# Token rows into expert order: indirect transfers and transposes in place of one-hot products

## What is computed

```python
x = _layernorm(DN_ALPHA * x + mod[2] * mixer(h), ln_g[l, 0], ln_b[l, 0])
h = x * (1.0 + mod[4]) + mod[3]
gsel = argmax(h @ w_group + b_group)                       # one group per token
top_p, top_i = top_k(softmax(elog of that group), 2)       # two experts in it
comb = sum(one_hot(eid, 32) * gw * top_p)
hid = silu(h @ w_gate[e]) * (h @ w_up[e]) * comb
moe = sum over e of hid @ w_down[e]
x = _layernorm(DN_ALPHA * x + mod[5] * moe, ln_g[l, 1], ln_b[l, 1])
```

## Time and profile before

| | us |
|---|---|
| median of three runs | 1325.98 |
| lowest, highest | 1325.22, 1329.46 |
| profiled execution, its own time | 1328.31 |
| its span, first to last instruction | 1326.1 |
| mean granted TensorE clock | 0.958 of full |

### The profile page before, as it was taken

How to read it: one execution, slowest core, us unless ns; L and a number is a source line. 1 busy time by engine, 2 the same in 40 slices (tenths; PEclk the granted TensorE clock), 3 DMA queues, 4 the chain that set the end, 5 groups by cost and what they waited for, 6 DMA issues and landing times.

```text
span 1326.1 us, 13297 instructions
## 1 busy us (share of the span) xinstructions
PE 1198.8 (90%) x4570; PEld 519.6 (39%) x4570; DVE 472.1 (36%) x1151; ACT 229.4 (17%) x422; POOL 91.9 (7%) x156
## 2 busy tenths in 40 slices
PE   4898999989899999999869799979879999999983
PEld 0343444435543333333334454544543333333331
DVE  1162322334713333333355132235461333333335
ACT  0252212221220000000023242242311000000001
POOL 4000000002110000000040000002300000000002
PEclk9798999999799999999979899989888999999997
DMA  9818455554709999999640321211603999999961
GB/s 374 351 54 318 185 237 216 206 212 158 318 16 362 382 379 381 385 389 380 271 191 32 133 79 67 88 40 72 250 3 127 375 384 382 380 384 378 374 233 69
DMA packets 47366, 318.80 MB, mean 240 GB/s; under 512 B 5856, under 2 KB 6960, under 8 KB 10464
## 3 DMA queue, kind: packets, MB, share of 16 engines
q1 hardware_dynamic: 43376, 299.92, 57.7%
q0 software_dynamic: 3200, 14.59, 2.9%
q10 hardware_dynamic: 752, 3.78, 0.8%
HBM read 314.54 MB, written 3.73 MB: 240 GB/s over the span
## 4 chain that ended last, share of the span: by engine, by line
PE 79%; DMA 9%; DVE 5%; ACT 4%; issue 2%; SPq 1%; POOL 0%; ACTq 0%; DVEq 0%; PEldq 0%
PE bank L616 37%; PE bank L958 16%; PE bank L984 11%; PE bank L975 8%; DMA ring<-in_w_moe 5%; DMA ring<-in_w_mod 3%; PE bank L637 2%; DMA ring<-in_w_in 1%; PE bank L1001 1%; PE bank L967 1%; PE bank L919 1%; PE bank L1021 1%; DVE region L1573 1%; DVE lstat L1515 1%; ACT hT L1317 1%
## 5 line engine op out<-in xcount | busy, mean ns | idle before, releaser
L958 PE MATMUL bank<-ring,region 128*64 128x512 f32 x1024 | 236.4, 605 | 6.3 <-issue 6.1
L984 PE MATMUL bank<-region 128*128 128x512 f32 x384 | 173.3, 601 | 0.0
L616 PE MATMUL bank<-ring,hT 128*128 128x512 f32 x384 | 171.5, 599 | 0.0
L616 PE MATMUL bank<-region 128*128 128x384 f32 (+8 forms) x584 | 135.2, 436 | 21.7 <-DVEq L1862 12.9
L958 PEld LDWEIGHTS bank<-ring,region 128*64 128x64 f32 x1024 | 69.6, 138 | 147.5 <-issue 147.5
L975 PE MATMUL bank<-ring,region 128*64 128x512 f32 x512 | 115.8, 594 | 5.3 <-DMA ring<-in_w_moe 5.2
L984 PEld LDWEIGHTS bank<-region 128*128 128x128 f32 x384 | 70.3, 190 | 102.5 <-issue 102.5
L616 PEld LDWEIGHTS bank<-region 128*128 128x128 f32 (+3 forms) x584 | 69.6, 179 | 92.7 <-issue 38.5
L616 PEld LDWEIGHTS bank<-ring,hT 128*128 128x128 f32 x384 | 71.0, 190 | 88.2 <-issue 87.7
L1932 DVE TENSOR_TENSOR region<-bank,region 128x512 f32<-128x512 f32 x128 | 82.4, 686 | 47.5 <-PE bank L975 47.5
L616 PE MATMUL bank<-hT,ring 128*128 128x384 f32 x256 | 91.5, 510 | 4.7 <-DMA ring<-in_w_in 4.7
(11 more groups left out here) (290 smaller groups left out, 917.1 us busy)
## 6 DMA issues: line engine op xcount, KB each, us to landing
ring<-in_w_moe SPq DMA_DIRECT2D x201, 1024.0 KB, 9.0
ring<-in_w_mod SPq DMA_DIRECT2D x48, 1024.0 KB, 10.5
ring<-in_w_in SPq DMA_DIRECT2D x24, 1024.0 KB, 9.8
ring<-in_w_out SPq DMA_DIRECT2D x4, 1024.0 KB, 7.4
ring<-in_w_out SPq DMA_DIRECT2D x8, 512.0 KB, 5.3
region<-gate_store POOLq DMA_DIRECT2D x4, 1024.0 KB, 6.3
region<-in_lnrows POOLq DMA_DIRECT2D x4, 1024.0 KB, 8.7
region<-row_store ACTq DMA_DIRECT2D x4, 768.0 KB, 4.2
```

What stands on the lines that cost most here:

```text
L616: ins = pe.matmul(out, lhsT, rhs, start=start, stop=stop, skip_group_check=True)
L958: ins = pe.matmul(bank[6][u * CAP:(u + 1) * CAP, :], xs[:, k, u * CAP:(u + 1) * CAP], ring[:, u, j, at:at + 2 * DE], start=k == 0, stop=k ...
L984: ins = pe.matmul(bank[2 * t + y][:, :], cwp[:, t * P:(t + 1) * P], ysb[:, min(t, 1), y * HALF:(y + 1) * HALF], start=False, stop=False, s ...
```

## The change

`route` stays, but ACT now also stores each block of `htok` into a DRAM tensor, `h_store`, after its two copies. `sel` becomes bf16. TensorE multiplies `sel` by a column of token numbers (`tokid`, shifted by 192 so that bf16 holds them) and gets, for each slot, the number of its token. DVE turns them into integers (`toki`), and POOL issues six indirect transfers, each of which brings 128 rows of 4 KB from `h_store` in slot order (`xrows`: the three blocks of `htok`, the two of `ysb`, and `xlast`). TensorE transposes each 128x1024 block in eight transposes, and ACT copies four at a time into `xg`. Three of the six input sums in layer 0 and four in layer 1 move from `experts` to the head of `gather` (`EARLY_SUMS`). The list product goes last, and DVE's work on its result goes behind the copy for pair 0. POOL's `bring_rows` for the next norm comes behind the six transfers. In the last norm DVE does the left half as well, and SP waits for the right half first. Ranks move from bank 5 to bank 7.

```diff
+EARLY_SUMS = (((1, 0), (1, 1), (2, 1)), ((1, 0), (1, 1), (2, 0), (2, 1)))
...
+            def gather_rows(l):
+                pool.wait_ge(S["h_out"], 16 * NT * (l + 1))
+                for b in range(SC):
+                    if b % NT == 0:
+                        pool.wait_ge(S["tok_sb"], 2 * l + b // NT + 1)
+                    pool.indirect_dma_start(out=xrows[b], out_offset=None, in_=h_store[l][:, :],
+                                            in_offset=bass.IndirectOffsetOnAxis(ap=toki[:, b:b + 1], axis=0)).then_inc(rows_at[b], 16)
...
                 affine(2 * l)
+                gather_rows(l)
...
-            for t in range(NT):
-                pool.wait_ge(S["hat_a"], 3 * NT + t + 1)
-                own(pool.tensor_tensor(xtok[:, t, 0:HALF], ztok[:, t, 0:HALF], ln_row[:, 0, 0:HALF], ALU.mult))
-                pool.tensor_tensor(xtok[:, t, 0:HALF], xtok[:, t, 0:HALF], ln_row[:, 1, 0:HALF], ALU.add).then_inc(S["y_a"], 1)
...
             def gather(l):
+                add_input(l, EARLY_SUMS[l])
                 for q in range(2):
                     pe.wait_ge(S["slots"], 2 * l + q + 1)
-                    for k in range(KD):
+                    if q == 1:
+                        pe.wait_ge(S["tok_sb"], 2 * l + 1)
+                    for i in range(NT):
+                        c = slice((q * NT + i) * P, (q * NT + i + 1) * P)
+                        for t in range(NT):
+                            ins = mm(bank[6][:, i:i + 1], sel[:, t, c], tokid[:, t:t + 1], t == 0, t == NT - 1)
+                    ins.then_inc(S["tok_ps"], 1)
+                if l == 0:
+                    mod_turn(1, 2)
+                for s in range(SC):
+                    pe.wait_ge(rows_at[s], 16 * (l + 1))
+                    for q in range(2):
                         b = pj()
-                        for t in range(NT):
-                            ins = mm(b[:, 0:N], htok[:, t, k * P:(k + 1) * P], sel[:, t, q * N:(q + 1) * N], t == 0, t == NT - 1)
+                        for k in range(4):
+                            ins = pe.transpose(b[:, k * P:(k + 1) * P], xrows[s][:, (4 * q + k) * P:(4 * q + k + 1) * P], ident[:, :])
                         ins.then_inc(S["pj_ready"], 1)
...
+                    if s == NT - 1:
+                        pe.wait_ge(S["diag_ready"], l + 1)
...
+                    act.wait_ge(S["pj_free"], n_pj[0])
+                    act.dma_start(h_store[l][t * P:(t + 1) * P, :], htok[:, t, :]).then_inc(S["h_out"], 16)
...
+                    dve.wait_ge(S["hat_a"], x * NT + t + 1)
+                    own(dve.tensor_tensor(xtok[:, t, 0:HALF], ztok[:, t, 0:HALF], ln_row[:, 0, 0:HALF], ALU.mult))
+                    dve.tensor_tensor(xtok[:, t, 0:HALF], xtok[:, t, 0:HALF], ln_row[:, 1, 0:HALF], ALU.add).then_inc(S["y_a"], 1)
...
+                def tokens_of(q):
+                    dve.wait_ge(S["tok_ps"], 2 * l + q + 1)
+                    c = slice(q * NT, (q + 1) * NT)
+                    own(dve.tensor_scalar(tokf[:, c], bank[6][:, 0:NT], float(N // 2), None, ALU.add))
+                    dve.tensor_copy(toki[:, c], tokf[:, c]).then_inc(S["tok_sb"], 1)
```

More of the change, by code:

```diff
@@ L312, in backbone_step @@
         offi = sb("offi", [1, NE], I32)
+        tokid = sb("tokid", [P, NT], BF16)
+        tokf = sb("tokf", [P, SC])
+        toki = sb("toki", [P, SC], I32)
+        xrows = [htok[:, t, :] for t in range(NT)] + [ysb[:, s, :] for s in range(2)] + [xlast]
         xrow = [hT[0:MAXL, 2 + i, 0:MAXJ * NE].rearrange("p (a b) -> p a b", a=MAXJ) for i in range(5)]
@@ L335, in backbone_step @@
         spread_in = [sem(f"spread_in{b}") for b in range(2)]
+        rows_at = [sem(f"rows_at{b}") for b in range(SC)]
         out_state = [sem(f"out_state{b}") for b in range(2)]
@@ L355, in backbone_step @@
         row_store = nc.dram_tensor("row_store", [H, 2, 2, N], F32).ap()
+        h_store = [nc.dram_tensor(f"h_store{l}", [N, D], F32).ap() for l in range(DEPTH)]
         gate_store = nc.dram_tensor("gate_store", [2 * DEPTH, 2, D], F32).ap()
@@ L951, in gather @@
+                pe.wait_ge(S["list_col"], l + 1)
+                pe.matmul(bank[7][:, 0:3 * MAXL], ones[0:MAXL, :], xdiag[:, :, :].rearrange("p a b -> p (a b)"),
+                          start=True, stop=True, skip_group_check=True).then_inc(S["list_row"], 1)
                 pe.wait_ge(S["pj_free"], n_pj[0])
@@ L986, in add_pair, with add_input @@
                 ins.then_inc(sig, 1)
-            def add_input(l):
-                pe.wait_ge(S["x_new"], NT * (2 * l + 1))
-                for t in range(NT):
-                    for y in range(2):
-                        pe.matmul(bank[2 * t + y][:, :], alpha_i[:, :], xtok[:, t, y * HALF:(y + 1) * HALF],
-                                  start=True, stop=False, skip_group_check=True)
+            def add_input(l, sums):
+                for t, y in sums:
+                    pe.wait_ge(S["x_new"], NT * 2 * l + t + 1)
+                    pe.matmul(bank[2 * t + y][:, :], alpha_i[:, :], xtok[:, t, y * HALF:(y + 1) * HALF],
+                              start=True, stop=False, skip_group_check=True)
             def extra_up(j, sig):
@@ L1069, in experts @@
                 up_second(0)
-                add_input(l)
+                add_input(l, [s for s in itertools.product(range(NT), range(2)) if s not in EARLY_SUMS[l]])
                 up_first(1)
@@ L1841, in _ @@
                 dve.wait_ge(S["ranks"], l + 1)
-                own(dve.tensor_copy(cnt[:, :], bank[5][:, NT * NE:(NT + 1) * NE]))
+                own(dve.tensor_copy(cnt[:, :], bank[7][:, NT * NE:(NT + 1) * NE]))
                 own(dve.tensor_tensor_scan(cums[:, :], ones[:, 0:NE], cnt[:, :], 0.0, ALU.mult, ALU.add))
@@ L1958, in _ @@
                 dve.wait_ge(S["xg_ready"], l + 1)
+                bring_x(0)
+                dve.wait_ge(S["list_row"], l + 1)
+                own(dve.tensor_copy(xlist[:, 0:MAXL], bank[7][:, 0:MAXL]))
+                own(dve.tensor_scalar(xlist[:, MAXL:2 * MAXL], bank[7][:, MAXL:2 * MAXL], float(NS), None, ALU.add))
+                behind(dve.tensor_copy(xlisti[:, 0:2 * MAXL], xlist[0:1, :]))
+                behind(dve.tensor_copy(xlisti[:, 2 * MAXL:2 * MAXL + 1], xcount[:, :]))
+                own(dve.tensor_scalar(colx[:, :], xlist[:, 0:MAXL], float(CAP), colw[:, 0:1], ALU.mult, ALU.add))
+                own(dve.scalar_tensor_tensor(out=colx[:, :], in0=bank[7][:, 2 * MAXL:3 * MAXL], scalar=float(FAR // CAP), in1=colx[:, :],
+                                             op0=ALU.mult, op1=ALU.add))
+                dve.sem_inc(S["lists"], 1)
                 dve.wait_ge(S["rows_in"], 32 * (2 * l + 2))
-                bring_x(0)
                 dve.wait_ge(S["qrow_ready"], l + 1)
```

66 lines of the change are left out of this document (28 added, 38 removed).

## The result

| | before | after |
|---|---|---|
| median, us | 1327.49 (4 runs, 1325.22 to 1329.46) | 1296.56 (4 runs, 1294.30 to 1299.27) |
| ratio to before | | 0.9767, 95% interval 0.9745 to 0.9789 |
| profiled execution, its span | 1328.31, 1326.1 | 1299.27, 1297.5 |
| mean granted TensorE clock | 0.958 | 0.943 |

The account below looks back on a forecast made before the run. TensorE, busy 1198.8 of 1326.1 us, and its chain of waits before the experts bound the kernel. 15.8 + 14.1 + 0.5 - 2.2 + 0 = 28.2 us off 1328.3 gives 1300.1, or 1298 against the median; range 1287 to 1312.

Parts of the forecast that it names:

- The stores: Ahead of the slots: three DMA issues in ACT's list cost 1.1 us per layer, bounds 0.35 and 3.0.
- The first rows: Gather, layer 1: first row transfer landed 5.5 us after the first half of the slots, bounds 2.5 and 9.2.
- The blocks: Gather: a block of eight transposes takes 1.8 us, from a clock of 0.53 in route; six blocks.
- upper clock: Rival, gather: early sums raise the clock, blocks take 1.3 us, start at 21; about 37 us gained, 1289; chance 0.13.
- The sums: Input sums moved into the idle before the slots: 0.5 us gained in layer 1, 0 in layer 0.
- The clock loss: Layer 0, pair 0 to pair 1's second half: up products start at a low clock, as in layer 1; 2.2 us lost.
- The end: Last norm: DVE takes over POOL's two passes and ends about where POOL did; 0, bounds -1.5 and +1.5.
- The expert rounds: Experts' pair rounds: expected unchanged.
- Rows late: Rival, gather: slow POOL issues or layer 0's traffic delay starts 3 to 8 us; 15 to 22 gained, 1308; chance 0.17.
- POOL held by DVE: Rival, gather: POOL cannot issue until DVE's work ends at 16.7 us; 1326; chance 0.04, shared with the no-change rival.
- Serial transfers: Rival, gather: each row transfer begins when the last has landed; 19.6 us worse per layer, 1365; chance 0.04.
- The change gives the start back: Rival, experts: the weight stream alone sets the stage, the earlier start is waited for; no change; shared chance 0.04.

Follow-up runs that it names:

- e5: Changed kernel without stores and row transfers, TensorE transposing the token blocks of htok directly: 1292.42 us, ratio 0.9739 to the kernel before.
- e6: Changed kernel with POOL waiting for each row transfer to land before issuing the next: 1323.11 us, ratio 0.9973 to the kernel before.
- e1: Changed kernel with the last norm as before, POOL's two small transfers behind its passes: 1300.91 us, ratio 0.9813 to the kernel before.
- e3: Changed kernel with no early sums, all six input sums behind pair 0's up products: 1295.97 us, ratio 0.9768 to the kernel before.
- e7: Changed kernel with the remaining input sums moved to the end of gather, ahead of pair 0: 1294.13 us, ratio 0.9757 to the kernel before.
- e8: As e7, plus seven repeated sums as filler in the wait for the first rows: 1294.51 us, ratio 0.9753 to the kernel before.
- e2: As e1, but POOL issues its two small transfers ahead of its passes: 1296.92 us, ratio 0.9773 to the kernel before.
- e4: Changed kernel with plain transfers of the same size in place of the six indirect ones: 1294.19 us, ratio 0.9770 to the kernel before.

## Why the prediction was right, point by point

| step (two numbers: layer 1, layer 0) | forecast, us | measured, us |
|---|---|---|
| stores, delay of the slots | 1.1 per layer | 0.6, 0.5 (against e5) |
| first rows, layer 1, layer 0 | 5.5, some 7.6 | 7.1, 9.5 |
| three blocks | 5.4 | 5.9, 5.2 |
| start of the last three blocks | 14.8, 16.9 | 16.2, 18.1 |
| last three blocks and copy | 6.2 | 4.6, 4.6 |
| experts start | 23.4, 25.5 | 23.2, 25.6 |
| gain up to there | 15.8, 14.1 | 17.4, 14.9 |
| pair 0 to pair 1's second half | +0.5, -2.2 | +0.8, -2.8 |
| rest of the expert rounds | 0 | -1.05, -2.8 |
| the end | 0 | +2.9 |
| other stretches | 0 | +0.7, -1.45 |

The mechanism is the one forecast: the products are gone, what is won at the start of the experts stays won but for some 2 us at pair 1, and the slower rivals did not come. That the total agrees to 0.4 us is luck in part. Rows that came 1.6 us late were made up by blocks that ran faster than forecast, the end gained what the forecast had at nothing, and the trace after holds some 3 to 4 us in the expert rounds that other executions of the same instructions don't.

**The stores** cost 0.6 and 0.5 us, half of what was forecast, as e5 shows. Their issues take 0.33 us each, as the earlier trace rows said. The third one counts in full (0.37), and the first two, hidden for the most part between copies, add some 0.2. Against the kernel before this does not show: from the first copy to the slots it is 12.80 us against 13.06 in layer 1 and 13.13 against 12.90 in layer 0, since ACT's copies followed each other more closely after (five steps from the first to the last in 3.84 us instead of 4.46 in layer 1). The table's row on the gain has the stretch as it differs from before, +0.3 and -0.2.

**The first rows** were 1.6 us later than forecast. `toki` was there at 1.5, as worked out, but POOL begins 0.8 us later, issues for 1.19 and the rows land 3.6 us behind that: 5.6 behind `toki`, where 3.9 was taken. The missing terms are POOL's start behind a semaphore (0.8, put at nothing) and the landing (3.6 where 2.9 was worked out from the earlier trace rows); the issue with its list, 1.19, was put at 1.0. The Trainium skill's fit in DMA: Bandwidth & Descriptors, section Anatomy of one DMA, gave 3.2 us for the 512 KB as an estimate. Counted from the end of POOL's issue, e6's transfers alone on their way land after 3.2 to 3.6 us (5.9 for the first of layer 0), so the trace agrees with it there; it leaves out the issue, and with several under way the recorded landings are 6.2 to 7.0 us behind the issues.

**The blocks.** The first three cost what the lower clock says. For the last three the forecast kept 1.8 us, and they took 1.1 to 1.2, set by ACT's two copies (a round of 1.41 us), because the clock had come up. It was not the `diag` products that brought it up: it rose while the third block was transposed, ahead of them, after 4.6 us of transposes in layer 0 and some 5.6 in layer 1. e5 shows the same in layer 1, with 0.50 from 954.2 to 957.0 and 1.00 from 958.0 to 959.1, where TensorE had only transposed since 954.3; in e1's layer 1 it rose at 970.6, within the `diag` products. The forecast kept the lower level for all six blocks, by the clock of 0.53 in `route`; that was the wrong step here. So part of the rival *upper clock* came true, for half of the blocks and not because of the early sums: it was priced as a whole, when the level changes inside the stage. This made up 1.6 us in each layer and hides the late rows, which is why the starts agree to 0.2 us. The Trainium skill, TensorE: Matmul & The Clock Gate, Part 4: PE-mode transpose, says that the upper level does not engage for transposes; here the clock rose to 1.00 while transposes ran, and eight took 1.08 us at it, so the measurement decides against the page.

**The sums** are worth nothing that can be told (0.5 was forecast), as e3 shows, and for the reason given: pair 1's weights are asked for when pair 0's up products end. **The clock loss** in layer 0 was foreseen by its cause and sized at 2.2; it is 2.8. The gap before pair 0 causes a good part of it: with that gap filled, e7 takes back 1.4 us and e8 2.6.

**The end** is the step that failed outright: 0, with bounds of 1.5, against 2.9. The forecast compared when DVE and POOL finish their lists. It overlooked that POOL's two small transfers moved ahead and that the span runs on for 4.2 us behind such an issue in the trace before (4.7 in e1), 2.4 behind SP's last one. e1 and e2 put some 2 us on that, and about 1 on DVE's passes.

**The expert rounds** were forecast unchanged, and lost 3.9 us in the trace after. This is not a cost of the change: e1 has the same instructions there, and its trace has 254.8 us in layer 0 and 254.7 in layer 1, as before (254.9 and 255.0); e2 has 254.1 and 256.1. In the trace after, 1.7 us of the 2.8 in layer 0, and more than the 1.05 in layer 1, are in one place, the last pair's down product. TensorE waits 2 us there for weights in both kernels; before, it went on at the upper clock,

```profile
652.53 3.65 PE L975 MATMUL bank<-ring,region 128*64 128x512 f32 x16 [1.95 <-DMA ring<-in_w_moe]
```

after, at 0.68:

```profile
640.89 5.32 PE L1004 MATMUL bank<-ring,region 128*64 128x512 f32 x16 [2.05 <-DMA ring<-in_w_moe]
```

It is 3.65 us behind such waits in both layers of e1 and e5, 5.3 in both of e3, e6 and e8, and one of each in e2, e4 and e7. After, e1 and e2 run the same instructions there and differ, so this is a cost that comes and goes from one execution to the next; which condition decides stays open, as do the remaining 1.1 us in layer 0's rounds. The 1.45 between the layers comes and goes too: e1 has 0.4 us less there than before, e2 1.6 more.

**The rivals.** *Rows late*: the issues took 0.95 and not 2 to 3 us, and TensorE waited no more behind the third block. The rival's price had a slip: a start 3 to 8 us later in each layer leaves 12 to 22 us of the 28.2, not 15 to 22. *POOL held by DVE*: POOL issued six times while DVE worked nearly without a break (961.58 to 969.0), and an issue took 0.94 us as it does in e6 with DVE idle, so what slows DVE beside POOL's arithmetic does not reach POOL's issues. For arithmetic e1 shows it again: DVE's three operations on `lnb_t` in the last norm take 0.16, 0.96 and 1.03 us with POOL's passes beside the latter two, 0.16 each without. DVE is not slowed there but held: in the kernel before, in e1 and in e2, two of the three take that long, and each of these six ends within 0.02 us of the end of POOL's pass. *Serial transfers*: e6 built it. 4.6 us per transfer is below the threshold of 5.4, and the experts do start sooner than before, but half of that is lost again at pair 1 and 0.3% is left. *The change gives the start back*: it did not, except for the 2.8 us at pair 1 of layer 0.

## What to carry to other kernels

A product whose matrix only selects rows can go out through memory and come back sorted, if several transfers are under way at once: here 34 us of products in each layer became 7 to 9 us of waiting and 9 to 10 of transposes. When a solid stage is replaced by waits, price the clock on both sides of each wait, inside the stage and in the one behind it; and before filling a gap ask what the next stage waits for, since sums moved there were worth nothing. At a program's end, look at which small transfer is issued last, and put it ahead of the arithmetic. And before a few us between two traces are put down to a change, look at the same stretch in a second trace of the same instructions: here the expert rounds differ by 3 to 4 us so.

## What the runs showed that was not expected

- Issues: an indirect transfer of 128 rows of 4 KB takes POOL 0.94 to 1.19 us and 0.30 until the next, a plain one 0.53; POOL starts an indirect one 0.8 us behind DVE's signal (a plain one 0.54 in e4), and 0.25 behind the landing of a transfer in e6.
- Six of them overlap: the last three of each layer take 6.2 to 7.0 us to landing, one per 1.3 us; plain ones issued every 0.53 us land no closer. One alone repeats every 4.6 us.
- Eight transposes take 1.97 us at a granted clock of 0.50, behind a wait, and 1.04 to 1.21 at 1.00; the clock reached 1.00 while nothing but transposes ran.
- A small DVE operation beside a POOL pass ends when the pass ends: 0.96 to 1.03 us instead of 0.16.
- A transfer of a few bytes from POOL as the last issue keeps the span open for 4.2 to 4.7 us, SP's last 256 KB for 2.4 to 2.7.
- The same wait of 2 us for weights leaves the next 16 products at 3.65 us in some executions and 5.3 in others, with the same instructions.
